# One-core transformer block: late sums moved into the index-score stage, slot weights moved into the expert steps, slot tables built in whole-block passes

## Time and profile before

| | us |
|---|---|
| median of 3 runs | 1877.51 (1873.25 to 1878.08) |
| the profiled execution's own time | 1871.25 |
| its span from first to last instruction | 1869.2 |
| PE busy | 1590.5 (85%) |
| DVE busy | 1384.6 (74%) |
| ACT busy | 719.4 (38%) |
| POOL busy | 166.1 (9%) |
| mean granted TensorE clock, share of full | 0.924 |

### The profile page before, as it was taken

How to read it: one execution, slowest core, us unless ns; L and a number is a source line. 1 busy time by engine, 2 the same in 40 slices (tenths; PEclk the granted TensorE clock), 3 DMA queues, 4 the chain that set the end, 5 groups by cost and what they waited for, 6 DMA issues and landing times.

```text
span 1869.2 us, 19950 instructions
## 1 busy us (share of the span) xinstructions
PE 1590.5 (85%) x6662; PEld 1030.3 (55%) x6662; DVE 1384.6 (74%) x1878; ACT 719.4 (38%) x819; POOL 166.1 (9%) x171
## 2 busy tenths in 40 slices
PE   3999999999999999467897596379999999999950
PEld 2446554444454455334554353268888888888840
DVE  6323997999698875576678532679999999999948
ACT  4000770000100011121333241067777777777733
POOL 0000000000111111100000000021011011010025
PEclk8999999999999999597999798589999999999975
DMA  9049102111000000952111011389999999999946
GB/s 375 5 176 380 75 12 101 68 46 45 1 6 12 6 6 6 357 193 74 61 46 46 12 40 57 114 338 422 419 411 418 409 413 415 413 412 413 394 157 248
DMA packets 85248, 355.31 MB, mean 190 GB/s; under 512 B 7873, under 2 KB 12097, under 8 KB 60609
## 3 DMA queue, kind: packets, MB, share of 16 engines
q1 hardware_dynamic: 56384, 268.51, 36.2%
q0 software_dynamic: 11776, 44.04, 6.3%
q10 hardware_dynamic: 17024, 41.95, 5.9%
HBM read 295.75 MB, written 58.72 MB: 190 GB/s over the span
## 4 chain that ended last, share of the span: by engine, by line
PE 72%; DVE 16%; DMA 4%; issue 3%; ACT 3%; POOL 1%; SPq 0%; DVEq 0%; POOLq 0%; ACTq 0%
PE PS L1435 16%; PE PS L1515 12%; PE PS L1659 9%; PE PS L1661 9%; PE PS L1660 9%; PE PS L1619 6%; DVE ACC L972 4%; PE PS L1654 1%; PE PS L1540 1%; PE PS L1553 1%; PE PS L1566 1%; DVE WK L891 1%; PE PS L1631 1%; DVE WK L1008 1%; DVE wlo L1313 1%
## 5 line engine op out<-in xcount | busy, mean ns | idle before, releaser
L1313 DVE TENSOR_TENSOR wlo<-raw,whi 128x2048 fp32r<-128x2048 f32 x192 | 435.9, 2285 | 45.6 <-ACT whi L784 44.8
L784 ACT ACTIVATE whi<-raw 128x2048 fp32r<-128x2048 f32 x192 | 363.4, 1911 | 55.3 <-DVE WK L1332 44.4
L1435 PE MATMUL PS<-BIG 128*128 128x512 f32 (+1 forms) x640 | 240.6, 531 | 2.0 <-ACT WK L697 2.0
L1515 PE MATMUL PS<-BIG 128*128 128x512 f32 x512 | 221.5, 593 | 0.7 <-ACT KV L684 0.7
L1659 PE MATMUL PS<-whi,xhi 128*128 128x512 f32 x512 | 203.4, 397 | 7.3 <-DVE wlo L1313 6.5
L1661 PE MATMUL PS<-whi,xlo 128*128 128x512 f32 x512 | 200.5, 392 | 0.0
L1660 PE MATMUL PS<-wlo,xhi 128*128 128x512 f32 x512 | 199.9, 390 | 0.0
L987 DVE MAX8 m<-KV 128x8 f32<-128x384 f32 (+5 forms) x192 | 171.6, 894 | 8.7 <-issue 2.6
L1435 PEld LDWEIGHTS PS<-BIG 128*128 128x128 f32 x640 | 110.8, 191 | 114.4 <-issue 111.6
L988 DVE MATCH_REPLACE8 KV<-m,KV 128x384 f32<-128x384 f32 (+5 forms) x192 | 168.1, 875 | 0.0
L1515 PEld LDWEIGHTS PS<-BIG 128*128 128x128 f32 x512 | 96.7, 190 | 120.9 <-issue 118.6
(11 more groups left out here) (247 smaller groups left out, 2036.9 us busy)
## 6 DMA issues: line engine op xcount, KB each, us to landing
raw<-in_w_gate SPq DMA_DIRECT2D x64, 1024.0 KB, 8.1
raw<-in_w_up SPq DMA_DIRECT2D x64, 1024.0 KB, 8.0
raw<-in_w_down SPq DMA_DIRECT2D x64, 1024.0 KB, 7.0
y_dram<-zero ACTq DMA_DIRECT2D x8, 3072.0 KB, 13.8
BIG<-in_w_in SPq DMA_DIRECT2D x8, 2048.0 KB, 10.8
BIG<-in_w_ada POOLq DMA_DIRECT2D x8, 2048.0 KB, 10.9
y_dram<-WK ACTq DMA_DIRECT2D x32, 512.0 KB, 7.6
BIG<-in_w_ada SPq DMA_DIRECT2D x3, 2048.0 KB, 19.1
```

Of the source, the lines that this page charges most:

```text
L784: nc.scalar.activation(whi[:, slot], raw[:, q], ACT.Copy).then_inc(G("m_hi"), 1)
L1313: V.tensor_tensor(wlo[:, slot], raw[:, q], whi[:, slot].bitcast(F32), ALU.subtract)\
L1435: last = mm(PS[:, u % 4, 0:w], hT[:, k, tile(t)], weights[:, k, 0:w], start=(k == 0), stop=(k == KD - 1))
L1515: last = mm(PS[:, k, :], hT[:, d, tile(t)], wb[k][:, d, :], start=(d == 0), stop=(d == KD - 1))
```

## The change

- **Late sums.** The products for the late rows are made by PE during the index scores. After every 12th score unit (LATE_EVERY, first at u = 6) comes `late_products(n)`, n = 0 to 7: eight matmuls with a column of c repeated 32 times as weights, four of them side by side in the four 32-partition groups of bank 6 or 7. POOL loads 2 MB for each, in two transfers, into one buffer, and the load of n waits until product n - 1 is done. ACT copies the two banks once, with scale 1/32. DVE's 64 operations are gone. In stage C `("late", m)` is now eight short items (one half row each): four in tile 0, two in tile 1, and gt2's two in tile 7.
- **Order.** `mix` and `norm` of tile 0 are finished in tile 1. `spend` takes nothing in tiles 0 to 3 at the heads, 2.4 at those of tiles 4 to 6, and 7.0 instead of 5.0 at each mix half. What is left of the search is forced at `("heads", (6, 6, 8))`. SP loads queries and `w_o` one round earlier, and the bias rows of gt1, sc2, g and sh2 in one go. PE forms the first logits ahead of the last retention tile, and DVE reads them there. gt2 has another place in memory, so that it can be loaded once the search is done.
- **Slots.** The two tables come from whole-block comparisons (8 x 128 and 16 x 50 elements at a time), and a third column, the slot's weight, comes with them. POOL copies the weight column of each step to `wcol`. The weight enters the product of silu(gate) and up; gt2 enters the eviction, which is one DVE operation of 1024 columns instead of a half each on ACT and DVE. Empty slots get an index out of bounds, and the gather leaves their rows out. POOL clears both gather buffers once. The final stage keeps one addition of the two results, and ACT's scaling, DVE's scaled addition and the product with gt2 are gone.

The diff, cut to its core:

```diff
-MIX_SPEND = 5.0
-HEADS_SPEND = (2.4, 3.2, 0, 0, 0, 0, 0, 0)
+MIX_SPEND = 7.0
+HEADS_SPEND = (0, 0, 0, 0, 2.4, 2.4, 2.4, 0)
...
+NO_TOKEN = 4096
...
-        gt2 = sb("gt2", [P, D])[:, :]
+        sb("spare3", [P, D])
+        gt2 = KV[:, 9216:10240]
...
-        late_sum = [BIG[:, a:a + 512] for a in (17408, 17920)] + [WK[:, 512 * m:512 * m + 512] for m in range(4)]
+        ada_late = WK[:, 5904:10000].rearrange("p (a k c) -> p a k c", a=2, k=2)
+        late_sum = [WK[:, a:a + 512] for a in (8704, 9216)]
...
-        between[0] = [[], [], [], []]
-        between[1] = [[], [], [("mix", (0, 0))], [("mix", (0, 1))]]
-        between[2] = [[("late", 1), ("late", 2), ("norm", 0)], [("turn", 0), ("mix", (1, 0))],
-                      [("route", 0), ("mix", (1, 1))], [("norm", 1)]]
-        between[3] = [[("turn", 1), ("mix", (2, 0))], [("route", 1), ("mix", (2, 1))], [("norm", 2)], [("turn", 2)]]
+                       [("turn", i - 1)]] for i in range(3, T)}
+        between[0] = [[("late", m)] for m in range(4)]
+        between[1] = [[("late", 4)], [("late", 5), ("mix", (0, 0))], [("mix", (0, 1))], [("norm", 0)]]
+        between[2] = [[("turn", 0), ("mix", (1, 0))], [("route", 0), ("mix", (1, 1))], [("norm", 1)], [("turn", 1)]]
+        between[T - 1][2].append(("late", 6))
...
-                if t == T - 1:
+                if t == T - 2:
...
+            sp.dma_start(WC["sc2"], b_sc2).then_inc(G("ld_c"), 16)
+            sp.dma_start(WC["g"], g_ffn).then_inc(G("ld_c"), 16)
+            sp.dma_start(WC["sh2"], b_sh2).then_inc(G("ld_c"), 16)
...
+                if i == T - 1:
+                    sp.wait_ge(G("topk_done"), len(SCORED))
+                    sp.dma_start(gt2, b_gt2).then_inc(G("ld_gt2"), 16)
...
+            for n in range(LATE_STEPS):
+                group, k = divmod(n, 4)
+                pool.wait_ge(*((G("late_used"), n) if n else (G("a_proj"), T)))
+                for a in range(2):
+                    pool.dma_start(ada_late[:, a], wada_v[:, LATE[2 * group + a][1], 2 * k:2 * k + 2])\
+                        .then_inc(G("ld_late"), 16)
...
+            pool.wait_ge(G("c_ytr"), T)
+            pool.wait_ge(G("b7_ready"), len(uses7))
+            own(nc.gpsimd.memset(WM["Xg"], 0.0), G("xg_clear"))
...
+                    bounds_check=S - 1, oob_is_err=False).then_inc(G(f"ld_rows{s}"), 16)
+
+            def take_weight(i, s):
+                column = tw[:, i:i + 1] if known(i, PEELED + 1) else tw[:, bass.ds(i, 1)]
+                nc.gpsimd.tensor_copy(wcol[:, s:s + 1], column).then_inc(G("m_w"), 1)
...
+                    if not known(i, 1):
+                        pool.wait_ge(G("m_h"), i)
+                    take_weight(i + 1, 1 - s)
...
+            for group in range(2):
+                act.wait_ge(G("late_used"), LATE_STEPS)
+                own.go(A(late_sum[group], PS[:, 6 + group, :], ACT.Copy, scale=1.0 / 32), G("late_sum"))
...
-                nc.scalar.activation(WM["Y"][:, s, 0:512], PS[:, 5, :], ACT.Copy).then_inc(G("m_ya"), 1)
...
-                act.wait_ge(G(f"f_y{t % NF}"), 32 * (t // NF + 1))
-                y1 = WF["y1"][t % NF]
-                own(A(y1, y1, ACT.Copy, scale=sw[:, 0, t:t + 1]), G("f_scaled"))
...
-                if t == T - 1:
-                    negated_logits(0)
-                    negated_logits(1)
...
+            dve.wait_ge(G("b_qr"), T)
+            dve.wait_ge(G("b_y"), T - 1)
+            negated_logits(0)
+            negated_logits(1)
...
-                    if i == T - 2 and lo == 0:
-                        for _ in last_pieces:
+                    if i == T - 2 and lo == HA - 2:
+                        for _ in pieces:
...
-                    sum_up(2 * i + 2)
-                    dve.wait_ge(*{"gt1": (G("ld_c"), 16 * 2), "sc2": (G("ld_sc2"), 16 * 2),
-                                  "sh2": (G("ld_sh2"), 16), "gt2": (G("ld_gt2"), 16)}[row])
...
+                    row, h = LATE[i // 2][0], i % 2
+                    dve.wait_ge(*((G("ld_gt2"), 16) if row == "gt2" else (G("ld_c"), 16 * 5)))
+                    part = slice(512 * h, 512 * h + 512)
+                    dst = (gt2 if row == "gt2" else WC[row])[:, part]
+                    dve.wait_ge(G("b7_ready"), at7[("late", i, 0)] + 1)
+                    if row == "sc2":
+                        own(V.scalar_tensor_tensor(dst, PS[:, 7, :], 1.0, dst, ALU.add, ALU.add), G("b7_free"))
+                        own(V.tensor_tensor(dst, dst, WC["g"][:, part], ALU.mult))
+                    else:
+                        own(V.tensor_tensor(dst, PS[:, 7, :], dst, ALU.add), G("b7_free"))
                 if kind == "rows":
...
-                own.go(V.tensor_scalar(WR["ohp"][:, n % 2], c("iota"), WR["r"][:, e, t:t + 1], None, ALU.is_equal))
-                own.go(V.tensor_scalar(WR["ohi"][:, n % 2], c("iota")[:, 0:64], WR["q"][:, e, t:t + 1],
-                                       c("token")[:, t:t + 1], ALU.is_equal, ALU.mult), G("r_oh"))
...
+            ohp, ohi = WR["ohp"], WR["ohi"]
+            own.go(V.tensor_tensor(ohi[:, :, 1], c("iota")[:, 0:TBL].unsqueeze(1).to_broadcast([P, 16, TBL]),
+                                   q16.unsqueeze(2).to_broadcast([P, 16, TBL]), ALU.is_equal))
             own.wait()
-            dve.wait_ge(G("r_acc"), 2 * T)
-            own(V.tensor_copy(tbl[:, :], PS[:, 2, 0:TBL]), G("r_done"))
+            for e in range(2):
+                own.go(V.tensor_tensor(ohi[:, 8 * e:8 * e + 8, 0], ohi[:, 8 * e:8 * e + 8, 1],
+                                       c("token").unsqueeze(2).to_broadcast([P, T, TBL]), ALU.mult))
+            own.go(V.tensor_tensor(ohp[:, 0:8], c("iota").unsqueeze(1).to_broadcast([P, 8, P]),
+                                   r16[:, 0:8].unsqueeze(2).to_broadcast([P, 8, P]), ALU.is_equal))
+            own.wait()
+            for e in range(2):
+                own.go(V.tensor_tensor(ohi[:, 8 * e:8 * e + 8, 1], ohi[:, 8 * e:8 * e + 8, 1],
+                                       sw[:, e, :].unsqueeze(2).to_broadcast([P, T, TBL]), ALU.mult),
+                       G("r_oh") if e == 0 else None)
+            own.go(V.tensor_tensor(ohp[:, 8:16], c("iota").unsqueeze(1).to_broadcast([P, 8, P]),
+                                   r16[:, 8:16].unsqueeze(2).to_broadcast([P, 8, P]), ALU.is_equal), G("r_oh"))
+            dve.wait_ge(G("r_acc"), 1)
+            own(V.tensor_copy(tw[:, :], PS[:, 2, TBL:2 * TBL]))
...
-                V.tensor_copy(WM["Y"][:, s, 512:1024], PS[:, 6, :]).then_inc(G("m_yd"), 1)
+                V.tensor_tensor(WM["Y"][:, s], PS[:, 5:7, :].rearrange("p b c -> p (b c)"), gt2, ALU.mult)\
+                    .then_inc(G("m_yd"), 1)
...
-                V.tensor_tensor(WM["h"], WM["hs"], PS[:, 3, :], ALU.mult).then_inc(G("m_h"), 1)
+                dve.wait_ge(G("m_w"), i + 1)
+                V.scalar_tensor_tensor(WM["h"], WM["hs"], wcol[:, s:s + 1], PS[:, 3, :], ALU.mult, ALU.mult)\
+                    .then_inc(G("m_h"), 1)
...
-                own(V.scalar_tensor_tensor(y1, y2, sw[:, 1, t:t + 1], y1, ALU.mult, ALU.add))
-                own(V.tensor_tensor(y1, y1, gt2, ALU.mult))
+                own(V.tensor_tensor(y1, y1, y2, ALU.add))
...
+            def late_products(n):
+
+                group, k2 = divmod(n, 4)
+                pe.wait_ge(G("ld_late"), 32 * (n + 1))
+                for k in range(2):
+                    for a in range(4):
+                        last = mm(PS[32 * a:32 * a + 32, 6 + group, :], cc[:, 2 * k2 + k:2 * k2 + k + 1].to_broadcast([P, 32]),
+                                  ada_late[:, a // 2, k, 512 * (a % 2):512 * (a % 2) + 512],
+                                  start=(k2 == 0 and k == 0), stop=(k2 == 3 and k == 1))
+                last.then_inc(G("late_used"), 1)
...
+                if u % LATE_EVERY == LATE_EVERY // 2:
+                    late_products(u // LATE_EVERY)
...
+            query_keys(0, 0)
...
-                    for h in range(2):
-                        pe.wait_ge(G("late_sum"), 2 * i + h + 1)
-                        bank7(("late", i, h))
-                        mm(PS[:, 7, :], ones[:, :], late_sum[(2 * i + h) % 6], start=True, stop=True)\
-                            .then_inc(G("b7_ready"), 1)
+                    rows = slice(32 * (i % 4), 32 * (i % 4) + 32)
+                    pe.wait_ge(G("late_sum"), 2)
+                    bank7(("late", i, 0))
+                    mm(PS[:, 7, :], ones[rows, :], late_sum[i // 4][rows, :], start=True, stop=True)\
...
+                if n % T == 0:
+                    pe.wait_ge(G("r_oh"), n // T + 1)
+                last = mm(PS[:, 2, 0:2 * TBL], WR["ohp"][:, n], WR["ohi"][:, n].rearrange("p a n -> p (a n)"),
+                          start=(n == 0), stop=(n == 2 * T - 1))
+            last.then_inc(G("r_acc"), 1)
```

155 lines of the change are left out of this document (41 added, 114 removed).

## The result

| | before | after |
|---|---|---|
| median of the runs, us | 1876.35 | 1842.03 |
| fastest to slowest run | 1873.25 to 1878.08 | 1841.51 to 1845.44 |
| the profiled execution's own time | 1871.25 | 1845.44 |
| ratio after to before, 95% interval | | 0.9823 (0.9804 to 0.9841) |

The account below looks back on a forecast made before the run. The prediction held that the pace-setting engine changes by stage, with PE the bound in the expert steps. Stage C's -51 us, with +5, 0, +1 and -6 elsewhere, stayed -51 and gave 1824 us, own range 1808 to 1842.

Parts of the forecast that it names:

- Tile 6 and tile 2: Stage C: tile 6 without forced pieces and late sums -34 us; tile 2 without late work and norm of tile 0 -17.
- Start of C and tile 1: Stage C's start: earlier loads against a new wait, 0 us; tile 1: late operations out, search pieces in, -2.
- the list at the end: Signs to check: tiles 1 to 7 of stage C at 37, 39, 40, 52, 38, 41 and 46 us between denominators.
- so 8 us: Start of stage C: DVE's new wait at tile 0's first late item until five transfers have landed, 8 us.
- Tile 7: Stage C: two late items add +0.5 us; behind the tile, gt2's bias loaded long before gives -6.5.
- Tiles 4, 5 and 6: Stage C: tile 4 with fourteen search pieces, bound by DVE at 52 us, +12; tile 5 without its six -4; tile 6 -34.
- Index scores: Late products on PE at 2.5 us each, one-deep loads leaving DVE without work in the first two intervals: +5 us.
- Tables and steps: Tables of slots by wide comparisons, 0 us; expert steps stay with PE, +1 us.
- Final stage: Last stage: DVE would save 11 us, but POOL's pace and reloads of x1 leave -6 us.
- products in a row: Rival, index scores: products run one after the other in PE, 6.9 us each, +20 instead of +5; 1839, chance 0.08.
- The search is only moved: Rival, stage C: PE stands still for tile 4's added pieces, +34 instead of +12; 1846, chance 0.04.
- The slower case: Rival, expert steps: POOL's copy takes 2.22 us a step from DVE, 81 us in all; 1905, chance 0.04.

Follow-up runs that it names:

- search_as_before: The changed kernel with search pieces behind the heads of tiles 0 and 1, as the kernel before had them, none in tiles 4 to 6; 1845.65 us, ratio 0.9853.
- all_four: The changed kernel with gt2's row earlier, no search pieces behind tile 4's heads, attention rows and first yb earlier, second late buffer held back; 1807.92 us, ratio 0.9654.
- final_rows_at_once: The changed kernel with eight buffers instead of four for the rows of x1 in the last stage, all loaded at its start; 1842.24 us, ratio 0.9837.
- no_weight_copy: The changed kernel with POOL's copy of a slot weight left out of all expert steps but the first; 1842.95 us, ratio 0.9835.
- serial_products: The changed kernel with a late product's four matmuls on all 128 columns of PE, one after the other; 1885.07 us, ratio 1.0062.
- two_late_buffers: The changed kernel with a second buffer for the late products' weights, so loads need not wait for the product before; 1850.91 us, ratio 0.9883.

## Why the prediction was right, and where it was off

The direction held. The time lies inside the range 1802 to 1848 that takes in the rivals, and at the very edge of the forecast's own range, 1808 to 1842; 1824 was 18 us too low. By its own steps:

- **Tile 6 and tile 2** were read rightly: with the forced pieces and the late sums gone they lost 31 and 18 us, forecast 34 and 17. search_as_before keeps the old table for the heads and still has 33 of the 37 us up to tile 6's end; which part of the rest of the change gives them is not divided.
- **Start of C and tile 1**: the sum of -2 came out, by luck, with two errors of opposite sign: against the list at the end tile 1 took 39.5 and not 37, and the stretch to rows(0) 38.9 and not the 41.4 that is left of the sum. The five rows were on the chain, 6.66 us, as the term "so 8 us" had them.
- **Tile 7** is the step that failed: "The load now waits for the search, in the memory of the search itself, and is there long before". The search was over at 979, but the load stands in SP's queue behind the waits for tile 6's mix and norm, was issued at 1101.2, and DVE waited for it until 1106.8. I had counted what it waits for and not what it is queued behind. It cost 9 us by the medians, part of it through the clock.
- **Tiles 4, 5 and 6**: DVE was tile 4's bound, but 56.1 us and not 52, since a piece beyond six cost 2.0 us and not the 1.5 I had given it. For tile 5 the step "Between tiles 3 and 7 PE's busy time grows by 1.5 us per tile" was wrong twice: with clock 1.00 it grows by 2.5, and the six pieces taken away had been free. -4 was +0.8, and tile 6 was short of its -34 by 2.7 for the same reason.
- **Index scores**: "I take 2.5" was pessimistic (1.85), and yet the term was too small, +9.5 for +5. I had laid the cost on DVE's shortfall behind late loads, and put the products' time on PE at nothing once the loads kept up. PE's records covered 91.2 of 93.2 us before already, though the chain lay on DVE; with the products in it the chain lies on PE. Making six products short gave back 4.5 us, and a second buffer 1.8 (2.9 in all_four).
- **Tables and steps**: -0.7 and +0.9 against 0 and +1. PE's weight loads waited for `hlo` for 0.8 us in all 32 steps, as before; the step stayed at 17.76.
- **Final stage**: -2.6 for -6. DVE's busy time fell by 10.4 us as said. As said too, POOL's pace and then a store and a reload of x1 took over, but I sized what they leave 3 us too low. final_rows_at_once shows that without the reload POOL's pace and DVE's end still hold the stage at 56.
- **Retention, +3.5**, was in no term. It is the dip of the clock, and no part of the change is shown to cause it.

Of the rivals, "products in a row" had the right price per product (6.9 us; measured 7.1) for a case that did not occur, but too low a total: +20 forecast, +50 measured against the scores of before (144.1 against 94.5, from DVE's first operation), as its sum took PE's own score products for covered. "The search is only moved" had +34 for tile 4; +16.0 came. The slower case, 2.22 us a step taken from DVE by POOL's copy, is refuted by no_weight_copy.

## What to carry to other kernels

Of every load that a change moves, read the queue it is issued from: what it stands behind matters more than what it waits for. Pieces of work on a side engine are free up to its slack in that tile and cost most of their length beyond (2.0 of 2.58 us here), so count them tile by tile and spread them evenly. When two engines are near full in a stage, work added to either shows.

## What the runs showed of the hardware

- Sixteen records of float32 matmuls over 512 columns take 1.85 us on four groups of 32 columns of PE, and 7.1 on all 128 columns (serial_products).
- A short wait of PE was followed by matmuls at half the granted clock, and cost more than its length: 6.18 us idle in tile 7 went with 17 us at the lower level and cost 12.6 by the profile; 2.95 us idle ahead of the scores (two_late_buffers) went with some 20 us at the lower level and cost 12.
- A copy of one value per partition on POOL takes 2.07 us beside DVE's subtraction of two SBUF operands, ending with it, and does not slow DVE.
- PE's clock also fell to 0.52 for some 7 us in the retention where PE had waited no more than at the same place of other tiles, in five of the thirteen profiles of changed kernels and not in the others.
